# Rows of the weight ring, the weight halves, the normalized input and the gated feed-forward tiles padded by 64 bytes

## The reference, cut to what matters

```python
def swiglu(x, w1, w3, w2):
    return (jax.nn.silu(x @ w1) * (x @ w3)) @ w2
...
h = h + 0.5 * swiglu(rmsnorm(h, norm_ffn1[i]), ffn1_w1[i], ffn1_w3[i], ffn1_w2[i])
z = rmsnorm(h, norm_mix[i]) @ w_in[i]
...
zc = split_cols(hc @ w_in[l], IN_SIZES)      # context, first layer only
... split_cols(h @ w_in[l], IN_SIZES)        # tokens
```

## Time and profile before

| | |
|---|---|
| median of 3 runs | 1575.96 us (1573.21 to 1578.48) |
| profiled execution, first to last instruction | 1577.9 us |
| PE busy | 95% |
| DVE, ACT, POOL busy | 60%, 46%, 8% |
| 16 DMA engines, mean of what they moved | 141 GB/s |

### The profile page before, as it was taken

How to read it: one execution, slowest core, us unless ns; L and a number is a source line. 1 busy time by engine, 2 the same in 40 slices (tenths; PEclk the granted TensorE clock), 3 DMA queues, 4 the chain that set the end, 5 groups by cost and what they waited for, 6 DMA issues and landing times.

```text
span 1577.9 us, 26099 instructions
## 1 busy us (share of the span) xinstructions
PE 1503.6 (95%) x10100; PEld 1333.2 (84%) x10100; DVE 939.9 (60%) x1478; ACT 728.2 (46%) x1257; POOL 120.5 (8%) x145
## 2 busy tenths in 40 slices
PE   6999999779999988999999999999999999999997
PEld 6999989659999987787777878888878887889997
DVE  5778878363777758775654437243334636556664
ACT  5444464265444446425544445222245536456444
POOL 3800000004000013001100100000000002010000
PEclk9999999899999999999999999999999999999999
DMA  8666645305767753452121212233332332225663
GB/s 295 217 203 197 210 159 163 124 28 195 245 228 251 241 185 108 144 184 86 54 74 60 68 67 93 94 113 101 108 106 79 115 101 81 81 94 176 206 204 122
DMA packets 74728, 223.25 MB, mean 141 GB/s; under 512 B 6672, under 2 KB 26128, under 8 KB 74128
## 3 DMA queue, kind: packets, MB, share of 16 engines
q1 hardware_dynamic: 54672, 195.20, 37.6%
q10 hardware_dynamic: 19968, 26.82, 5.1%
HBM read 220.94 MB, written 1.05 MB: 141 GB/s over the span
## 4 chain that ended last, share of the span: by engine, by line
PE 80%; DVE 8%; ACT 4%; DMA 4%; issue 2%; POOL 0%; DVEq 0%; SPq 0%; ACTq 0%
PE ps L495 67%; DMA ring<-stream 4%; PE ps L508 2%; DVE w_lo L427 2%; ACT w_hi L1219 2%; PE ps L959 1%; PE ps L975 1%; PE ps L967 1%; DVE area L1768 1%; PE ps L1043 1%; PE ps L1032 1%; PE ps L932 1%; DVE area L2143 1%; DVE mod_junk L1788 1%; PE ps L715 1%
## 5 line engine op out<-in xcount | busy, mean ns | idle before, releaser
L495 PE MATMUL ps<-hn_hi,w_hi 128*128 128x256 f32 (+1 forms) x1895 | 608.3, 321 | 21.7 <-DVE w_lo L427 7.0
L495 PE MATMUL ps<-hn_hi,w_lo 128*128 128x256 f32 (+1 forms) x1895 | 593.0, 313 | 0.0
L495 PE MATMUL ps<-hn_lo,w_hi 128*128 128x256 f32 (+1 forms) x1895 | 593.0, 313 | 0.0
L427 DVE TENSOR_TENSOR w_lo<-ring,w_hi 128x1024 fp32r<-128x1024 f32 (+1 forms) x331 | 395.9, 1201 | 305.1 <-ACT w_hi L1219 301.6
L1219 ACT ACTIVATE w_hi<-ring 128x1024 fp32r<-128x1024 f32 (+1 forms) x347 | 359.9, 1038 | 341.3 <-DMA ring<-stream 256.5
L495 PEld LDWEIGHTS ps<-hn_hi,w_hi 128*128 128x128 f32 x1895 | 361.8, 191 | 52.3 <-DVE w_lo L427 10.5
L495 PEld LDWEIGHTS ps<-hn_lo,w_hi 128*128 128x128 f32 x1895 | 362.1, 191 | 21.4 <-issue 1.2
L495 PEld LDWEIGHTS ps<-hn_hi,w_lo 128*128 128x128 f32 x1895 | 362.1, 191 | 21.2
L1287 ACT ACTIVATE area<-ps 128x512 f32<-128x512 f32 (+1 forms) x148 | 72.3, 503 | 216.4 <-PE ps L495 215.5
L495 PE MATMUL ps<-area_r,w_hi 128*128 128x256 f32 (+1 forms) x578 | 135.9, 329 | 1.0 <-DVE w_lo L427 0.5
L495 PEld LDWEIGHTS ps<-area_r,w_hi 128*128 128x128 f32 x578 | 96.1, 188 | 14.7 <-issue 2.8
(11 more groups left out here) (320 smaller groups left out, 1666.6 us busy)
## 6 DMA issues: line engine op xcount, KB each, us to landing
ring<-stream SPq DMA_DIRECT2D x359, 512.0 KB, 3.8
mod_at<-mod_stream ACTq DMA_DIRECT2D x34, 512.0 KB, 5.6
area<-mod_stream ACTq DMA_DIRECT2D x12, 512.0 KB, 5.4
pk<-pack ACTq DMA_DIRECT2D x1, 1610.0 KB, 7.0
pk<-pack SPq DMA_DIRECT2D x1, 1549.0 KB, 12.3
h<-x_in SPq DMA_DIRECT2D x1, 1024.0 KB, 4.9
cond_at<-cond SPq DMA_DIRECT2D x2, 512.0 KB, 14.1
mod_at<-mod_stream SPq DMA_DIRECT2D x2, 512.0 KB, 12.4
```

The source lines that it names most:

```text
L427: eng.tensor_tensor(lo[:, 0:w], raw, hi[:, 0:w].bitcast(F32), ALU.subtract).then_inc(lo_ready[who], 1)
L495: m = pe.matmul(dst, w_, x_, start=(start and n == 0), stop=(stop and n == 2), skip_group_check=True)
```

## The change

The rows of `ring`, `w_lo` and `w_hi` become 1040 columns long (4160 bytes) where they were 1024, those of `hn_hi`, `hn_lo` and of the two tiles that share their bytes 528 (2112 bytes) where they were 512, and those of `hid_hi` and `hid_lo` 272 (1088 bytes) where they were 256. The new 16 columns are neither written nor read. All accesses are cut to the old widths; no instruction, transfer or wait is added, removed or moved. The working area grows by 512 bytes, because its first pieces make room for the longer rows of `hid`.

```diff
-AREA = 25472
+AREA = 25600
+PAD = 16
...
-        with nc.sbuf_tensor("ring", [P, RING, UW], F32) as ring:
+        with nc.sbuf_tensor("ring", [P, RING, UW + PAD], F32) as ring:
             pass
-        w_lo = sb("w_lo", [P, RING, UW], F32R)
-        w_hi = sb("w_hi", [P, HI, UW], F32R)
+        w_lo = sb("w_lo", [P, RING, UW + PAD], F32R)
+        w_hi = sb("w_hi", [P, HI, UW + PAD], F32R)
...
-        with nc.sbuf_tensor("cond_at", [P, KT, 2 * T], F32) as cond_at:
+        with nc.sbuf_tensor("cond_at", [P, KT, 2 * T + PAD], F32) as cond_at:
             pass
-        hn_hi = sb("hn_hi", [P, KT, 2 * T], F32R)
-        with nc.sbuf_tensor("mod_at", [P, KT, 2 * T], F32) as mod_at:
+        hn_hi = sb("hn_hi", [P, KT, 2 * T + PAD], F32R)
+        with nc.sbuf_tensor("mod_at", [P, KT, 2 * T + PAD], F32) as mod_at:
             pass
-        hn_lo = sb("hn_lo", [P, KT, 2 * T], F32R)
+        hn_lo = sb("hn_lo", [P, KT, 2 * T + PAD], F32R)
...
-        with nc.sbuf_tensor("hid_hi", [P, 4, T], F32R) as hid_hi, nc.sbuf_tensor("hid_lo", [P, 4, T], F32R) as hid_lo:
+        with nc.sbuf_tensor("hid_hi", [P, 4, T + PAD], F32R) as hid_hi, nc.sbuf_tensor("hid_lo", [P, 4, T + PAD], F32R) as hid_lo:
...
-        cut(8 * T - Area.at)
+        cut(8 * (T + PAD) - Area.at)
...
-            return w_hi[:, SPLIT[name] % HI, :], w_lo[:, UNIT[name] % RING, :]
+            return w_hi[:, SPLIT[name] % HI, 0:UW], w_lo[:, UNIT[name] % RING, 0:UW]
...
-                sp.dma_start(ring[:, u, :], stream[u]).then_inc(unit_loaded[u], 16)
+                sp.dma_start(ring[:, u, 0:UW], stream[u]).then_inc(unit_loaded[u], 16)
```

More of the change, by code:

```diff
@@ L355, in merged_parts @@
             if l == 0:
-                return hn_hi[:, k, :], hn_lo[:, k, :]
+                return hn_hi[:, k, 0:2 * T], hn_lo[:, k, 0:2 * T]
             return early_hi[:, k, :], free_halves[k // 4][:, k % 4, T:2 * T]
@@ L464, in _ @@
                     sp.wait_ge(units_multiplied, RING * r + (u + 1 - RING))
-                    sp.dma_start(ring[:, u, :], stream[RING * r + u]).then_inc(unit_loaded[u], 16)
+                    sp.dma_start(ring[:, u, 0:UW], stream[RING * r + u]).then_inc(unit_loaded[u], 16)
             for u in range(rounds * RING, NU):
                 sp.wait_ge(units_multiplied, u + 1 - RING)
-                sp.dma_start(ring[:, u % RING, :], stream[u]).then_inc(unit_loaded[u % RING], 16)
+                sp.dma_start(ring[:, u % RING, 0:UW], stream[u]).then_inc(unit_loaded[u % RING], 16)
             sp.wait_ge(resid_ready, RESID_BLOCK2 + LAYERS * KT - KT // 2)
@@ L480, in unit @@
                 pe.wait_ge(unit_loaded[u % RING], 16 * (u // RING + 1) + 16 * rounds)
-                return ring[:, u % RING, :]
+                return ring[:, u % RING, 0:UW]
             def split_unit(name, body=0):
@@ L1243, in gated_high @@
                     act.wait_ge(s("gated"), count)
-                    act.activation(hid[0][:, f % 4, :], sil[:, f % 4, :], ACT.Copy).then_inc(s("hid_high"), 1)
+                    act.activation(hid[0][:, f % 4, 0:T], sil[:, f % 4, :], ACT.Copy).then_inc(s("hid_high"), 1)
                 base = SPLIT[tag, "w1", 0]
@@ L1880, in gated_low @@
                 def gated_low(f, count):
-                    v, hi, lo = sil[:, f % 4, :], hid[0][:, f % 4, :], hid[1][:, f % 4, :]
+                    v, hi, lo = sil[:, f % 4, :], hid[0][:, f % 4, 0:T], hid[1][:, f % 4, 0:T]
                     dve.wait_ge(s("hid_high"), count)
```

## The result

The changed kernel took 1583.16 us, median of 6 runs (1577.70 to 1587.08), the kernel before 1576.08 us beside it (6 runs, 1573.21 to 1578.48). The ratio is 1.0041, 95% interval 1.0025 to 1.0057: slower by 0.4%, +6.5 us, where I forecast 2.3 us less. A second series of the same code gave 1.0026 (1.0010 to 1.0042), +4.1 us. The time lies within the range as a whole (1560 to 1592) and just above that of the mixture (1567 to 1582); the direction is the other one.

A forecast was written before the change was run, and what follows sets the result against it. PE was taken to bound the kernel, busy 1503.6 of 1577.9 us, through the distance between matmul starts. Terms -12.4 + 4.8 + 6.3 - 1.0 = -2.3 us took 1575.96 to 1573.7 us; range 1560 to 1592.

The forecast's parts named there:

- the mixture: Main case: distances evenly mixed, half of them dear at both widths; -2.3 us, own range 1567 to 1582, chance 0.50.
- The durations depend on the distance of streamed row and weight block: PE's matmuls: 256 columns cost 119 ns at distance 0, 113 at 192; 512 columns 227 at 0, 233 at 192.
- it does nothing: Rival: the 6 ns hang on something else that goes with the tile, and the pads leave them; 1576 us, chance 0.14.
- The size of the step: Dear and cheap distances differ by 6 ns a matmul, multiplied by the matmul counts of each form.
- The change scatters the distances evenly: Streamed rows against weight slots: all eight multiples of 64, by 512, come up about equally often for hn, hid and area_r.
- Half of each distance is dear: Assumption for unseen distances at both widths, 6 ns a matmul: -12.4 + 4.8 + 6.3 - 1.0 = -2.3 us.
- 256 columns, hn: 4122 narrow matmuls streamed from hn: -24.7 us if all went cheap, 0 if none; forecast -12.4 us.
- 512 columns, hn and weights: 2091 wide matmuls streamed from hn or weight slots, cheap before: +12.5 us if all went dear; forecast +6.3 us.
- Other engines and transfers at nothing: DVE's address effect, bound 2.2 us, and transfers, landing in 3.8 us a unit, were both put at nothing.
- Only equal places collide: Rival: distance 0 alone is dear for narrow matmuls, the other seven behave like 192; -9.3 us, 1566.7, chance 0.22.
- The scatter itself costs: Rival: the cheap level needs one particular distance, so nearly every matmul goes dear; +22 us, 1598, chance 0.14.
- The means I named as signs: Group means: 256 columns from hn 283 to about 280 ns, hid and area_r 277 to 280; 512 from hn 391 to 394.

## Why the prediction was wrong, step by step

**What bounds the kernel:** right. PE has 81% of the chain, and time followed the distance between starts in nearly every run.

**The durations depend on the distance of streamed row and weight block:** right, and shown by moving one tile at a time. The Trainium skill speaks against it ("SBUF — State Buffer", section "Who interferes with whom": the two reads of TensorE, for the streamed operand and for the weight load, are independent of each other). Taken to hold for addresses too, that rule would have given all runs the paces of the kernel before; a 64-byte shift of w_hi alone cost 10.6 us of PE's busy time. The measurement decides. The rival "it does nothing" falls with it.

**The size of the step:** a little too large. I read 6 ns off two fast stretches; the pace over the whole run differs by 5.1 (119.7 against 114.6), because some stretches of hid (6 of 45 settled ones) ran at the slower beat and runs of hn start with steps below 120.

**The change scatters the distances evenly:** right for hn, where the timeline shows uneven steps. It is even for hid too over both layers, but from unit to unit: each w2 unit meets one row of hid, so the distances stay the same within it. It is not even for area_r: its rows were not padded and `w_hi` has three slots, so against `w_hi` only 128, 64 and 0 (by 256) come up and never 192. By the table these give 118.3 and 230.2 ns with the four places of `w_lo`; 118.2 and 231.8 came. Against an even mixture this changes the sum by less than 1 us.

**Half of each distance is dear:** this step failed, and it holds nearly all of the error. By its terms:

| | forecast, us | measured, us |
|---|---|---|
| 256 columns, hn | -12.4 | 4122 x -1.8 = -7.4 |
| 256 columns, hid and area_r | +4.8 | 3.2 + 2.0 = +5.2 |
| 512 columns, hn and weights | +6.3 | 6.7 + 1.7 = +8.4 |
| 512 columns, area_r | -1.0 | -0.5 |
| sum | -2.3 | +5.7 |

(+5.7 from these rounded terms, +5.8 unrounded.) Of the 8.0 us between them 5.0 are the gain of hn, which came at 1.8 ns instead of 3, and 2.1 the loss of the wide ones. Two things were wrong in it. First, the unseen distances are not half and half: at 256 columns three of four levels lie near the dear end (119.7, 117.6, 118.7 against 114.5 to 115.1), and at 512 two of four do. With the even mean of the four, 117.7 and 230.7, the sum would have been 4122 x -2.0 + 1056 x 3.1 + 534 x 3.3 + 1563 x 3.0 + 528 x 2.8 - 333 x 2.7 = +2.1 us, slower already. Second, a mixture can be dearer than its mean, as the run with w_hi moved showed on its own for hn. The changed kernel has 232.0 ns for 512 columns from hn where the even mean has 230.7; on 1563 matmuls that is 2.0 of the remaining 3.7 us. At 256 columns from hn it is only 117.9 against 117.7, 0.8 us on 4122 matmuls.

**Other engines and transfers at nothing:** right. The low and the high part of the changed kernel, and its landing of a unit, are those of the earlier trace rows:

```profile
L428 DVE TENSOR_TENSOR w_lo<-ring,w_hi 128x1024 fp32r<-128x1024 f32 x315 | 384.6, 1227 | 270.4 <-ACT w_hi L1220 266.9
...
L1220 ACT ACTIVATE w_hi<-ring 128x1024 fp32r<-128x1024 f32 x331 | 349.8, 1058 | 321.1 <-DMA ring<-stream 244.7 <-PE ps L496 66.6 <-issue 8.4
...
ring<-stream SPq DMA_DIRECT2D x359, 512.0 KB, 3.8
```

**The rivals.** "Only equal places collide" is wrong: 64 and 128 are nearly as dear as 0 at 256 columns. "The scatter itself costs" came nearest: at 256 columns the cheap level does need one particular distance, 192. At 512 two of four are cheap, and the mixing itself added little (1.3 ns for hn). I had given 0.14 to it, because I priced it at its end, +22 us, with no gain left for hn. Its turning point (three quarters dear at 256 columns, half at 512, +6.2 us) is close to what came. The levels of the earlier trace rows already spoke for it: two of three distances dear, at a third width.

**The means I named as signs** came out as 282 for hn at 256 columns (280 forecast), 280 for hid and 281 for area_r (280), and 394 for hn at 512 (394). They look nearly right, and the sign of the time was wrong: on 4122 matmuls 1 ns is 4.1 us, more than my whole forecast of 2.3. Rounded means can't carry such a sum; the busy times of the groups can.

## What to carry to other kernels

Where TensorE bounds a kernel with short float32r matmuls, each with its own weight load, the distance between the streamed row and the weight block, taken by 256 bytes, is worth up to 4% of a narrow matmul (119.7 against 114.5 ns). Measure the levels first, with an unused tile ahead of one operand, and then place each stage at its best one; padding rows by 64 bytes gave about the mean of the levels or worse (117.1 to 118.2 against 117.7 ns, 231.1 to 232.1 against 230.7), so it can pay only where the present distance is worse than that at the widths that matter. When a sum has terms of both signs that nearly cancel, its sign hangs on the term with the largest count, so that term needs a row of its own.

## What the runs showed of the hardware that I had not expected

- TensorE's pace depends on where the two operands lie to each other, which of its parts makes it so no run shows. The dependence has a period of 256 bytes, not 512, and the two widths want opposite places: 192 is the best for 256 columns (114.5 ns) and the worst for 512 (233.3), 0 the other way round (119.7 and 227.7).
- The direction counts: 64 and 192, the same distance with the sign turned, differ by 3 ns at 256 columns and by 4 at 512. Where weights are streamed, the level is that of the turned distance (229.6 with hn at 192, 233.3 with hn at 64).
- At a constant distance PE settles into a beat that is kept: 120 ns at 0, 117.8 at 64, a pattern of five steps of 118.7 in mean at 128. At 192 there are two, 113.3 and 117.8 ns, and each can last for hundreds of matmuls. A change from distance 0 to 192 without a pause led to the fast one in all 67 cases counted; a change of tile at the same distance kept the beat in 57 of 58.
- Matmuls at different distances that follow each other share one pace, in five of six cases worse than the mean of theirs (for hn 118.0 against 116.2, 232.9 against 231.4; the exception is area_r at 512 columns, 230.1 against 232.7).
